# Falling tile order and earlier reciprocals in the forgetting attention of a hybrid decoder block

## The reference

```python
def forgetting_attention(q, k, v, logf):
    scale = d ** -0.5
    c = jnp.transpose(jnp.cumsum(logf, axis=1), (0, 2, 1))
    for i in range(lp // BLOCK):
        q0, kend = i * BLOCK, (i + 1) * BLOCK
        s = jnp.einsum('bqhd,bkhd->bhqk', q[:, q0:kend], k[:, :kend]) * scale
        s = s + c[:, :, q0:kend, None] - c[:, :, None, :kend]
        mask = (kpos[None, :kend] <= qpos[:, None]) & (kpos[None, :kend] >= PAD)
        p = jax.nn.softmax(jnp.where(mask[None, None], s, NEG_INF), axis=-1)
        outs.append(jnp.einsum('bhqk,bkhd->bqhd', p, v[:, :kend]))
    return jnp.concatenate(outs, axis=1)
```

## Time and profile before

| | us |
|---|---|
| median of 3 runs | 3201.52 |
| lowest and highest | 3199.4, 3202.2 |
| the profiled execution | 3200.72 |
| its span, first to last instruction | 3198.9 |
| from the first turn to the last scatter of the forgetting attention | 937 to 1475 |
| output projection and experts | 1475 to 3199 |

### The profile page before, as it was taken

The page is one execution under the profiler, slowest core; times in us unless marked ns, Lnnn a source line. Parts: engine busy times, 40 slices in busy tenths (PEclk is TensorE's granted clock), DMA queues, the critical chain, the costliest instruction groups (busy, mean ns, idle before and its releaser), DMA issues.

```text
span 3198.9 us, 38064 instructions
## 1 busy us (share of the span) xinstructions
PE 3107.4 (97%) x14302; PEld 1999.1 (62%) x14302; DVE 1100.6 (34%) x3387; ACT 693.4 (22%) x1555; POOL 641.2 (20%) x631
## 2 busy tenths in 40 slices
PE   8999999999999889898999999999999999999997
PEld 4455555544445555454555777787777777777775
DVE  6423333330035656554677421111111111111115
ACT  2221111110024444452111101111111111111114
POOL 3200000000000010101354312222222222323225
PEclk9999999999999999999999999999999999999999
DMA  6421010011000102005444367888888788888886
GB/s 228 145 68 27 14 28 14 1 35 38 20 1 8 49 9 107 9 8 178 140 140 159 115 236 238 238 227 241 240 242 242 244 244 264 260 270 264 271 243 233
DMA packets 179112, 458.82 MB, mean 143 GB/s; under 512 B 24944, under 2 KB 97472, under 8 KB 153192
## 3 DMA queue, kind: packets, MB, share of 16 engines
q1 hardware_dynamic: 133872, 339.23, 29.8%
q0 software_dynamic: 42752, 108.72, 15.5%
q10 hardware_dynamic: 2304, 8.39, 0.7%
HBM read 342.33 MB, written 113.92 MB: 143 GB/s over the span
## 4 chain that ended last, share of the span: by engine, by line
PE 52%; DVE 1%; POOL 0%; issue 0%; ACT 0%; ACTq 0%; DVEq 0%
PE ps L2338 22%; PE ps L2282 11%; PE ps L2148 7%; PE ps L2266 4%; PE ps L2196 3%; PE ps L2279 2%; PE ps L2208 1%; PE ps L2168 1%; PE ps L2226 0%; PE ps L2158 0%; POOL moe_fin L1949 0%; PE ps L2135 0%; DVE moe_fin L1614 0%; PE ps L2181 0%; PE ps L2180 0%
## 5 line engine op out<-in xcount | busy, mean ns | idle before, releaser
L697 PE MATMUL ps<-ret_w,hT 128*128 128x512 f32 (+1 forms) x1088 | 465.0, 580 | 0.0
L2338 PEld LDWEIGHTS ps<-moe_xT,moe_wg 128*128 128x128 f32 x2048 | 352.7, 196 | 44.8 <-issue 40.7
L2338 PE MATMUL ps<-moe_xT,moe_wg 128*128 128x192 f32 (+22 forms) x2048 | 378.4, 338 | 0.0
L2338 PE MATMUL ps<-moe_xT,moe_wu 128*128 128x192 f32 (+22 forms) x2048 | 375.2, 336 | 0.0
L2282 PE MATMUL ps<-moe_wd,moe_hh 128*128 128x512 f32 (+12 forms) x800 | 366.5, 601 | 1.0 <-DVE moe_hh L1432 0.8
L2338 PEld LDWEIGHTS ps<-moe_xT,moe_wu 128*128 128x128 f32 x2048 | 353.3, 196 | 4.3
L697 PEld LDWEIGHTS ps<-ret_w,hT 128*128 128x128 f32 (+1 forms) x1088 | 195.5, 185 | 223.0 <-issue 215.9
L1890 POOL DMA_INDIRECT base_rows<-moe_yo,index x100 | 164.7, 1647 | 847.3 <-DVE moe_yo L1537 717.9
L1432 DVE TENSOR_TENSOR moe_hh<-moe_sl,ps 128x256 f32<-128x256 f32 (+19 forms) x144 | 53.8, 373 | 774.0 <-ACT moe_sl L2004 773.7
L2282 PEld LDWEIGHTS ps<-moe_wd,moe_hh 128*128 128x128 f32 (+12 forms) x800 | 136.6, 181 | 159.3 <-issue 149.8
L1053 PE MATMUL ps<-hT,fox_w 128*128 128x512 f32 (+1 forms) x576 | 226.9, 555 | 0.0
(11 more groups left out here) (252 smaller groups left out, 3591.3 us busy)
## 6 DMA issues: line engine op xcount, KB each, us to landing
moe_wg<-in_we_gate SPq DMA_DIRECT2D x64, 1024.0 KB, 4.9
moe_wu<-in_we_up SPq DMA_DIRECT2D x64, 1024.0 KB, 7.0
moe_wd<-in_we_down SPq DMA_DIRECT2D x64, 1024.0 KB, 7.8
fox_c<-ck SPq DMA_DIRECT2D x8, 1032.0 KB, 8.6
emb_xin<-in_x SPq DMA_DIRECT2D x16, 512.0 KB, 4.0
h_rows<-emb_hr SPq DMA_DIRECT2D x16, 512.0 KB, 2.8
ret_w<-in_w_in SPq DMA_DIRECT2D x16, 512.0 KB, 6.7
moe_yt<-h_rows SPq DMA_DIRECT2D x16, 512.0 KB, 4.9
```

Source lines behind the costliest of these rows:

```text
L697: ins = pe.matmul(ps[0:n, g % 2, lo:hi], hT[:, c, t0:t0 + n], wr[u][:, c, lo:hi], start=(c == 0), stop=(c == DC - 1))
L2338: ins = pe.matmul(out, w[:, c, f:FF:FC], xT[u][:, c, 0:n], start=(c == 0), stop=(c == DC - 1))
```

## The change

The tiles of each pass go in falling order of length. `inverse(n)` moves: in tiles 6 to 0 it stands right behind the copy of the first group, ahead of all biases of the next tile; in tile 7 it stands behind the copy of the group of i = 6, where before it stood at i = 3. SP waits for both halves of the stores to `foxT` before its first load of the expert stage, where before it waited for the second half after two loads.

```diff
-        order = [(p, t) for p in range(PAIRS) for t in (7, 6, 5, 4, 3, 1, 0, 2)]
-        assert len(set(order)) == PAIRS * TILES
+        order = [(p, t) for p in range(PAIRS) for t in range(TILES - 1, -1, -1)]
@@ block.vector of fox_phase
                 for s in groups[n][0]:
                     back(n, s)
+                if not HALF[n]:
+                    inverse(n)
                 for i in range(max(len(groups[n]), lead[n])):
                     for s in (groups[n][i + 1] if i + 1 < len(groups[n]) else []):
                         back(n, s)
+                    if HALF[n] and i == HALF[n]:
+                        inverse(n)
                     for u in (per(n + 1, i) if i < lead[n] else []):
                         bias(n + 1, u)
-                    if i == (3 if HALF[n] else min(1, len(groups[n]) - 1)):
-                        inverse(n)
                     if i == 1 and n >= 1:
                         finish(n - 1)
@@ block.sync of moe_phase
-            sp.wait_ge(ahead.fox_out[0], ahead.fox_stored[0])
+            for b in range(2):
+                sp.wait_ge(ahead.fox_out[b], ahead.fox_stored[b])
             feathers(0)
             hidden(0)
-            sp.wait_ge(ahead.fox_out[1], ahead.fox_stored[1])
```

## The result

| | before | changed | ratio, 95% interval |
|---|---|---|---|
| median, first measurement | 3200.46 | 3167.59 | 0.9897 (0.988 to 0.9914) |
| median, measured again with the kernels below | 3199.73 | 3167.72 | 0.9897 (0.988 to 0.9914) |
| the profiled execution | 3200.72 | 3168.89 | |
| its span | 3198.9 | 3167.1 | |

The forecast was 3167.2 with a range of 3161 to 3178. In the changed file the lines from L904 to L965 stand one lower than before: L904 is the bias and L910 that of the diagonal, L919 the maximum, L932 and L934 DVE's copies, L943 and L946 the reciprocals and their products, L954 finish. Those behind stand one higher: L1007 is ACT's exponential, L1065 the scores, L1084 and L1089 the turns, L1109 and L1116 the weighs, L1127 the scatter.

A forecast was written before the change was run, and what follows sets the result against it. PE, busy 97% of the span, bounds the kernel, so time comes only from its waits or clock. Gains of 7.9 + 26.4 = 34.3 us take the profiled 3200.72 to 3166.4; the median, 0.8 above, is 3167.2, range 3161 to 3178.

The forecast's parts named there:

- Tiles 3 to 0: New order and earlier reciprocals in these tiles gain 5.1, 6.9, 9.2 and 5.2 us in the four passes, sum 26.4.
- DVE starts when u0 is scored, 0.85 after PE: Tile 0: DVE begins its biases once PE has scored the first unit, 0.85 us after PE starts, and ends at 11.7.
- The waits in slices: Tile 0: the 2.89 us wait goes, and about 2 us in slices of 0.25 to 0.6 replace it.
- The turn behind the scatter: Tile 7's third turn, after tile 0's scatter, waits for DVE's copy, which starts 0.2 us later against the scatter.
- Tile 7: Moving its reciprocals from i = 3 to i = 6 gains 3.2 us of waits and 4.7 of clock, sum 7.9.
- The late copy: Tile 7: reciprocals ahead of the last copy make the last weigh some 0.4 us late per tile, bounds 0 and 1.28.
- the new wait of some 0.4: Sign in tile 7: a new PE wait of some 0.4 us before the last weigh.
- The clock: Low-clock windows between 937 and 1440 gone; gains of 11 us in tiles 3 to 0 and 4.7 in tile 7.
- rival 1: Tile 0: PE's waits in slices lower the clock at three pass ends, costing 5 to 12 us; 3172 to 3179; chance 0.14.
- Rival 2: Tile 7's wait is ACT's, as signed, so it and its low clock stay; 3176.7; chance 0.08.
- Rival 3: Tiles 6 to 0: reciprocals hold up the biases, up to 1.28 us a tile, and the clock stays low; 3218.6; chance 0.02.
- Rival 4: No gain: PE waits as long as before in tile 0 and tile 7's head, at low clock; about 3200; chance 0.03.

The follow-up runs named there:

- both fillers: Changed kernel with a useless DVE maximum over 1024 or 2048 columns behind the reciprocals of tiles 6 to 0; one execution each, stage 502.28 and 507.21 us.
- tile 7 undone: Changed kernel with tile 7's reciprocals back behind the biases of i = 3; 3168.45 us, ratio 0.9916 to before.
- the three kernels with more copies by ACT: Changed kernel with ACT copying one more group in tiles 7 to 3; then finish early too; then one copy fewer in tile 3: 3156.53, 3155.67, 3153.87 us.
- others undone: Changed kernel with the reciprocals of tiles 6 to 0 back behind the biases of i = 1; 3186.71 us, ratio 0.9966 to before.
- order alone: Changed kernel with all reciprocals back in their old places, keeping the falling tile order and SP's earlier wait; 3189.03 us, ratio 0.998 to before.
- the SP run: Kernel before with only SP's second wait moved ahead of its first load; one execution, 3197.49 us, stage 531.41.

## Why the prediction was right, point by point

- **The total**, 3167.2 against 3167.59, is closer than the working deserves. The stage gained 35.1 where the sum had 34.3, but the profiled execution came out at 3168.89 and not 3166.4, since 3.3 us were lost outside the stage, and the median lies 1.3 below that execution where it was put 0.8 above. That these misses cancel to 0.4 us is luck.
- **Tiles 3 to 0:** 26.4 forecast; measured 4.85 + 6.61 + 8.95 + 5.52 = 25.9. Tile by tile 13.4, 10.1 and 7.66 stood against 13.45, 10.00 and 7.59. Tile 0 was the one mis-sized: from the first scores to the scatter 10.2 was forecast, and it took 10.67 (1185.28 to 1195.95). The step is "DVE starts when u0 is scored, 0.85 after PE": it starts 1.13 after, and the earlier trace rows already had 1.10 (1181.88 less 1180.78). That is 0.28 of the 0.47: the run of DVE work itself took 10.82 (1186.41 to 1197.23), just the 10.8 of the sum, and behind a run that sets the end such a constant counts in full. The other 0.2 stays without a cause. The waits in slices were put at about 2 us in pieces of 0.25 to 0.6; the rows have 1.20 in pieces of 0.19 to 0.43, and PE was idle for 1.49 in all from the first scores on. The turn behind the scatter came no later than before (0.49 again, not 0.2 more), so tile 0 from its first scores on and this turn together miss by 0.3.
- **Tile 7:** 7.9 forecast, 9.2 measured: 1.12 in pass 1 and 2.7, 2.7 and 2.7. The wait fell to 0.73 (0.72 forecast). The late copy is the term that was mis-sized: it cost 0.1 and not 0.4. The merged weigh before the scatter takes 1.40 where it took 1.30, and the new wait of some 0.4 that was named as a sign did not come, as PE was still busy with the weighs before the last one. So the waits gave 4.5 where 3.2 stood, and the clock 4.7 as forecast.
- **The clock:** all eight low stretches in the stage are gone, as forecast, and rival 1 did not come. In tile 0 PE waits in slices and the granted clock stays 1.00 (2.4 GHz), in both profiles of the changed kernel and in those of both fillers (where single slices reached 0.75 and 1.01), tile 7 undone and the three kernels with more copies by ACT: 24 tiles 0 in all. So the Trainium skill's remark on short idles between matmul groups ("TensorE: Matmul & The Clock Gate", section "A second HAM failure mode: psum-queue depth-cycling") does not bite on waits of this size here. Larger ones do, sometimes: 1.94 in tile 7, 1.61 or 1.62 among the scores of tile 0 in others undone, and in order alone and before also two waits close together in tile 1.
- **Rival 2** (ACT releases tile 7's turn) fell with tile 7 undone. The argument against it was not quite right: the turn does wait on the semaphore of the exponentials (`exped` in `turn`), but for a count that the first turn of q = 1 had already waited for, six turns earlier. **Rival 3** did not come, and the fillers show where it would begin. **Rival 4** did not come.
- **What the prediction did not see:** that its base was one draw. It took 15.7 us of low clock out of one execution of before (11 in tiles 3 to 0, 4.7 in tile 7) as if they belonged to the kernel. Tile 7 undone had the same waits of 1.94 without any low clock behind them, and the second execution of the old stage was 5.7 us shorter. That the medians differ by 32.9 says that on the mean before pays much of it, but the split between waits (19.5) and clock (15.6) holds for that profile only. Likewise the changed profile lost 2.9 us to a low stretch in the retention stage, in code that nobody touched.
- **What stays open:** by what a wait of 1.9 us brings the low clock once and not the next time. No run here varied it alone. The same holds for the 1.6 of tile 0 in others undone and order alone.

## What to carry to other kernels

A wait names the last event before it, not the price: before you remove what a wait is signed by, look what else ends at the same time, since here, at the end of tile 0, moving the reciprocals alone only handed the wait on to the exponentials. Put short work that is needed late where its engine is idle anyway, and measure how much more fits there; put the work of a long tile into the short one before it only if the engine that then sets the pace has no stray work in that run. And when a term of a sum is clock, take it from more than one execution.

## What the runs showed of the hardware

- The same program with the same waits got low-clock stretches in one execution and not in another: 37 us of them in the stage of before and 24 in the second execution of it (the SP run). Behind the wait of 1.94 in tile 7 they came in three of four passes in each of these two, in one of four in order alone, and in none of four in tile 7 undone. Where one comes there it costs 1.5 to 1.6 us (28.60 to 28.74 against 27.11).
- It can come behind shorter waits. In pass 3 of before the last ones ahead of it were 1.07 and 0.64 us, apart by one weigh, and the turns that followed ran at 1.2 GHz. In others undone 0.98 and 0.64 at the same place of pass 1 brought nothing.

```profile
1314.19 0.44 PE L1108 MATMUL ps<-fox_pT,fox_v 128*64 128x128 f32 x4 [1.07 <-DVE fox_pT L933]
1315.27 0.82 PE L1126 MATMUL ps<-fox_rd,fox_onesf 128*64 128x128 f32 x8 [0.64 <-DVE fox_rd L947]
1316.02 2.40 PE L1083 MATMUL ps<-ident,hT 128*16 128x128 f32 x10
```

```profile
1315.60:1319.00 3.40, 3.40 (x20) 1.93 (x16) 0.69 (x1) 1.12 (x3) 0.00 (x0) 0.50 0.11 39
```

- In tile 0, a wait of 1.61 or 1.62 us among the scores, behind two shorter ones, had the clock fall at its end in two of six tiles (others undone and order alone).

- The waits of tile 0 in the new order, slices of 0.19 to 0.43 us and 1.20 in sum in the changed kernel, left the granted clock at 1.00 in all 24 tiles with waits of up to 1.01.
- With the waits equal and the clock high, tiles repeat to some 0.02 us from execution to execution, so single traces told differences of 0.1 us that the total's interval of some 5 us to either side can't.
